# Overflow groups moved ahead of the third group, and the next layer's query weights and product moved ahead of expert 28, in a two-layer mixture-of-experts trunk

## The reference, cut to what matters

```
u   = rms_norm(x) @ w_in                 # 1024 x 3328, first 512 columns: attention queries
x   = x + mixer(u) @ w_out               # attention, gated recurrence, short convolution
h   = rms_norm(x)
g   = best of 4 groups;  e1, e2 = best 2 of the 8 experts in it    # per token
x   = x + sum over e1, e2 of gate_e * ((silu(h @ w_gate[e]) * (h @ w_up[e])) @ w_down[e])
```

## Time and profile before

| | us |
|---|---|
| three runs | 1174.75, 1175.57, 1178.22 (median 1175.57) |
| the profiled execution, whole | 1178.1 |
| its span, first to last instruction | 1176.3 |
| mean granted TensorE clock | 0.904 of full speed |

### The profile page before, as it was taken

How to read it: one execution, slowest core, us unless ns; L and a number is a source line. 1 busy time by engine, 2 the same in 40 slices (tenths; PEclk the granted TensorE clock), 3 DMA queues, 4 the chain that set the end, 5 groups by cost and what they waited for, 6 DMA issues and landing times.

```text
span 1176.3 us, 21016 instructions
## 1 busy us (share of the span) xinstructions
PE 891.2 (76%) x8821; PEld 539.1 (46%) x8821; DVE 473.4 (40%) x1264; ACT 181.8 (15%) x508; POOL 43.3 (4%) x98
## 2 busy tenths in 40 slices
PE   9999998665757665648999999886666667565577
PEld 6577475332424332325575675643323233333244
DVE  2977474331313132323349674733223222232322
ACT  2334121100101010001223441111000000000001
POOL 2001120000000000000000120000000000000000
PEclk9999999897979797988999999987978797989888
DMA  8946589999999999999996275999999999999996
GB/s 277 380 197 244 221 351 426 426 427 427 428 428 428 430 428 429 426 428 417 417 387 264 72 279 199 374 426 427 426 428 427 428 430 428 428 428 430 427 425 271
DMA packets 56147, 442.32 MB, mean 376 GB/s; under 512 B 9472, under 2 KB 12560, under 8 KB 31248
## 3 DMA queue, kind: packets, MB, share of 16 engines
q1 hardware_dynamic: 56080, 441.37, 91.1%
HBM read 440.30 MB, written 1.05 MB: 375 GB/s over the span
## 4 chain that ended last, share of the span: by engine, by line
PE 53%; DMA 38%; DVE 5%; issue 2%; SPq 1%; ACT 0%; DVEq 0%; POOL 0%; POOLq 0%
DMA ring<-in_expert_w_up 38%; PE psum L969 14%; PE psum L1002 8%; PE psum L1013 6%; PE psum L983 5%; PE psum L1088 5%; PE psum L780 2%; PE psum L942 2%; DVE work L1727 1%; PE psum L819 1%; PE psum L1036 1%; PE psum L870 1%; SPq L493 1%; PE psum L1271 1%; PE psum L959 1%
## 5 line engine op out<-in xcount | busy, mean ns | idle before, releaser
L969 PE MATMUL psum<-ring,work 128*32 128x256 f32 x3712 | 257.0, 438 | 111.7 <-DMA ring<-in_expert_w_up 111.2
L969 PEld LDWEIGHTS psum<-ring,work 128*32 128x32 f32 x3712 | 143.9, 126 | 221.8 <-issue 173.3
L983 PE MATMUL psum<-ring,work 128*32 128x256 f32 x1664 | 128.2, 461 | 127.7 <-DVE work L1733 127.5
L1725 DVE TENSOR_SCALAR work<-work 128x128 f32<-128x128 f32 x62 | 14.5, 233 | 346.1 <-ACT work L1357 346.1
L983 PEld LDWEIGHTS psum<-ring,work 128*32 128x32 f32 x1664 | 57.5, 129 | 193.2 <-DVE work L1733 117.3
L1738 DVE COPY work<-psum 32x256 f32<-32x256 f32 x124 | 52.6, 424 | 139.7 <-PE psum L983 138.6
L1002 PE MATMUL psum<-ring,hT 128*128 128x512 f32 x208 | 91.0, 593 | 0.0
L1361 ACT ACTIVATE work<-psum 32x256 f32<-32x256 f32 x124 | 46.3, 373 | 266.4 <-PE psum L983 265.7
L1357 ACT ACTIVATE work<-psum 128x128 f32<-128x128 f32 x62 | 17.2, 278 | 364.4 <-PE psum L969 333.6
L1013 PE MATMUL psum<-hT,ring 128*128 128x256 f32 x320 | 70.8, 379 | 0.0
L942 PE MATMUL psum<-work 128*128 128x512 f32 x112 | 53.4, 621 | 15.1 <-DVE work L1738 15.1
(11 more groups left out here) (321 smaller groups left out, 837.1 us busy)
## 6 DMA issues: line engine op xcount, KB each, us to landing
ring<-in_expert_w_gate SPq DMA_DIRECT2D x64, 2048.0 KB, 18.1
ring<-in_expert_w_up SPq DMA_DIRECT2D x60, 2048.0 KB, 22.5
ring<-in_expert_w_down SPq DMA_DIRECT2D x52, 2048.0 KB, 22.0
ring<-in_w_in SPq DMA_DIRECT2D x10, 2048.0 KB, 18.8
work<-in_expert_w_down SPq DMA_DIRECT2D x6, 2048.0 KB, 15.0
ring<-in_w_out SPq DMA_DIRECT2D x4, 2048.0 KB, 8.1
maps<-in_expert_w_down SPq DMA_DIRECT2D x2, 2048.0 KB, 9.2
ring<-in_expert_w_up SPq DMA_DIRECT2D x4, 1024.0 KB, 30.7
```

The source lines that it names most:

```text
L969: last = T.matmul(bank[GU_BANK[i % 2]][CAP * j:CAP * j + CAP, 0:2 * P], xg[:, k, CAP * i:CAP * i + CAP], gate_up[:, :, k, P * j:P * j + P] ...
L983: last = T.matmul(bank[5][CAP * q:CAP * q + CAP, 0:2 * P], actT[i % 2][:, CAP * j:CAP * j + CAP], down[j][:, 2 * P * q:2 * P * q + 2 * P], ...
```

## The change

The overflow block moves on every engine from behind group 6 to behind group 1, so ahead of group 2. It then runs, where it runs, before the sums are final, and the copies and seeds that put them back are gone. ScalarE and VectorE have group 1 written out ahead of it and loop over groups 2 to 6.

SyncE issues the four loads of the next layer's query weights before the first load of expert 28, in place of behind its third.

On TensorE the whole product ahead of the first 128 tokens comes before expert 28's gate/up product, and that of the second 128 is split around expert 28's down and expert 29's gate/up product. `project_rest(0)` comes behind it, and a wait for its copy (`rest_sb`) stands in front of expert 30. ScalarE's copies follow that order.

The diff, without the removal of the signal `again_x` and of the parameter `seed` of `experts`:

```diff
@@ -589,26 +588,26 @@
                 part(ring_full, seven[1], 7, 1)
                 e.wait_ge(main.ye_ps.sem, main.ye_ps.after(first + 1, 1))
                 part(ring_full, seven[2], 7, 2)
+                count, prior = extra_groups(e, l)
+                with e.If(count > 0):
+                    with e.Fori(0, count) as t:
+
+                        e.wait_ge(main.scat_ps.sem, main.scat_ps.after(l * GROUPS + 2, 0))
+                        for i in range(UG):
+                            ex = e.value_load(xinfo[0:1, l:l + 1, ds(t * UG + (2 + i), 1)], min_val=0, max_val=NE - 1)
+                            unit(xring_full, extra, prior + t, i, ex)
+
+                        e.wait_ge(extra.scat_ps.sem, extra.scat_ps.after(prior + t, 4))
+                        settle(e)
                 with e.Fori(2, GROUPS - 1) as g:
                     for i in range(UG):
                         unit(ring_full, main, l * GROUPS + g, i, g * UG + i)
 
-                count, prior = extra_groups(e, l)
-                with e.If(count > 0):
-                    with e.Fori(0, count) as t:
-
-                        e.wait_ge(main.scat_ps.sem, main.scat_ps.after(l * GROUPS + GROUPS - 1, 0))
-                        for i in range(UG):
-                            ex = e.value_load(xinfo[0:1, l:l + 1, ds(t * UG + (2 + i), 1)], min_val=0, max_val=NE - 1)
-                            unit(xring_full, extra, prior + t, i, ex)
-
-                        e.wait_ge(extra.scat_ps.sem, extra.scat_ps.after(prior + t, 4))
-                        settle(e)
                 last = l * GROUPS + GROUPS - 1
+                if l < DEPTH - 1:
+                    first_section(l + 1)
                 for i in range(UG - 1):
                     unit(ring_full, main, last, i, (GROUPS - 1) * UG + i, LAST, 3)
-                    if i == 0 and l < DEPTH - 1:
-                        first_section(l + 1)
                 sg, su, sd = placed(l, LAST[UG - 1])
                 e.wait_ge(main.gu_ps.sem, main.gu_ps.after(last, UG - 3))
                 part(ring_full, sg, NE - 1, 0)
@@ -832,13 +831,14 @@
                 gate_transposes(S, turn, True)
                 if ahead:
                     sums_transposed()
-                    for n in range(TI):
-                        expert_units(S, turn, [("up", n)], slots, loaded)
-                        project_ahead(n, range(0, KT // 2))
-                        expert_units(S, turn, [("down", n)], slots, loaded)
-                        project_ahead(n, range(KT // 2, KT)).then_inc(ahead_q_ps.sem, 1)
-                        if n == 0:
-                            project_rest(0)
+                    project_ahead(0, range(0, KT)).then_inc(ahead_q_ps.sem, 1)
+                    expert_units(S, turn, [("up", 0)], slots, loaded)
+                    project_ahead(1, range(0, KT // 2))
+                    expert_units(S, turn, [("down", 0), ("up", 1)], slots, loaded)
+                    project_ahead(1, range(KT // 2, KT)).then_inc(ahead_q_ps.sem, 1)
+                    project_rest(0)
+                    expert_units(S, turn, [("down", 1)], slots, loaded)
+                    e.wait_ge(rest_sb.sem, rest_sb.after(l, 1))
                     expert_units(S, turn, [("up", 2)], slots, loaded)
                     project_rest(1)
                     expert_units(S, turn, [("down", 2)], slots, loaded)
@@ -931,10 +931,6 @@
                     gate_transposes(S, turn)
                     expert_units(S, turn, order, slots, loaded)
                 e.wait_ge(S.gat_sb.sem, S.gat_sb.after(turn, 1))
-                if seed:
-                    e.wait_ge(again_x.sem, again_x.after(turn, 4))
-                    for n in range(4):
-                        T.matmul(bank[SUM_BANK[n]][:, :], ident[:, :], x[:, n // 2, n % 2 * 512:n % 2 * 512 + 512], start=True, stop=False)
                 e.wait_ge(S.ye_act.sem, S.ye_act.after(turn, 4))
                 e.wait_ge(S.ye_dve.sem, S.ye_dve.after(turn, 4))
                 for n in range(4):
@@ -1276,14 +1272,14 @@
                 experts(main, l * GROUPS + 1, IN_TURN, second, unit_loaded(1))
                 more = l < DEPTH - 1
                 count, prior = extra_groups(e, l)
+                with e.If(count > 0):
+                    with e.Fori(0, count) as t:
+                        e.wait_ge(main.scat_ps.sem, main.scat_ps.after(l * GROUPS + 2, 0))
+                        experts(extra, prior + t, IN_TURN, later, lambda s, i: xring_full[s].after(prior + t, 16 * (i // 2 + 1)))
                 with e.Fori(2, GROUPS - 2 if more else GROUPS - 1) as g:
                     experts(main, l * GROUPS + g, IN_TURN, later, turn_loaded(g))
                 if more:
                     experts(main, l * GROUPS + GROUPS - 2, IN_TURN, later, turn_loaded(GROUPS - 2), final=True)
-                with e.If(count > 0):
-                    with e.Fori(0, count) as t:
-                        e.wait_ge(main.scat_ps.sem, main.scat_ps.after(l * GROUPS + GROUPS - 1, 0))
-                        experts(extra, prior + t, IN_TURN, later, lambda s, i: xring_full[s].after(prior + t, 16 * (i // 2 + 1)), more, more)
                 last_experts(l, l * GROUPS + GROUPS - 1, final, unit_loaded(GROUPS - 1))
 
 
@@ -1321,20 +1317,23 @@
                 e.wait_ge(S.gat_ps.sem, S.gat_ps.after(turn, 1))
                 A(gat_both, bank[7][:, :], ACT.Copy).then_inc(S.gat_sb.sem, 1)
                 if ahead:
+                    def part_out(t):
+
+                        e.wait_ge(ahead_q_ps.sem, ahead_q_ps.after(l, t + 1))
+                        A(part_q[t], bank[7][:, :], ACT.Copy).then_inc(ahead_q_sb.sem, 1)
+
+                    part_out(0)
                     for n in range(UG - 1):
                         expert_units(S, turn, [("up", n)])
-                        if n == 2:
-                            rest_out(1)
+                        if n == 1:
+                            part_out(1)
+                        if n:
+                            rest_out(n - 1)
                         e.wait_ge(S.ye_ps.sem, S.ye_ps.after(turn, n + 1))
                         if n:
                             e.wait_ge(yt_ok.sem, yt_ok.after(l, n))
                         A(flat[0:P // 2, :], bank[5][0:P // 2, 0:2 * P], ACT.Copy).then_inc(flat_ok.sem, 1)
                         expert_units(S, turn, [("down", n)])
-                        if n < TI:
-                            e.wait_ge(ahead_q_ps.sem, ahead_q_ps.after(l, n + 1))
-                            A(part_q[n], bank[7][:, :], ACT.Copy).then_inc(ahead_q_sb.sem, 1)
-                        if n == 0:
-                            rest_out(0)
                 else:
                     expert_units(S, turn, LAST_TURN)
                 e.wait_ge(gate_ps.sem, gate_ps.after(l, 1))
@@ -1526,18 +1525,14 @@
                 A(edif, edif, ACT.Exp).then_inc(exp_e.sem, 1)
 
                 experts(main, l * GROUPS, OVERLAPPED)
-
-                with e.Fori(1, GROUPS - 1) as g:
-                    experts(main, l * GROUPS + g, IN_TURN)
+                experts(main, l * GROUPS + 1, IN_TURN)
                 count, prior = extra_groups(e, l)
                 with e.If(count > 0):
                     with e.Fori(0, count) as t:
-                        e.wait_ge(main.scat_ps.sem, main.scat_ps.after(l * GROUPS + GROUPS - 1, 0))
-                        if l < DEPTH - 1:
-                            sums_to_x(again_x)
+                        e.wait_ge(main.scat_ps.sem, main.scat_ps.after(l * GROUPS + 2, 0))
                         experts(extra, prior + t, IN_TURN)
-                        if l < DEPTH - 1:
-                            e.wait_ge(extra.scat_ps.sem, extra.scat_ps.after(prior + t, 4))
+                with e.Fori(2, GROUPS - 1) as g:
+                    experts(main, l * GROUPS + g, IN_TURN)
                 last_experts(l, l * GROUPS + GROUPS - 1)
 
 
@@ -2178,12 +2173,13 @@
                 experts(main, l * GROUPS, OVERLAPPED, codes, l, l * (GROUPS - 1), extra_units, gate_values)
                 c.end()
                 e.wait_ge(c.sem, c.last())
-                with e.Fori(1, GROUPS - 1) as g:
-                    experts(main, l * GROUPS + g, IN_TURN, codes, l, l * (GROUPS - 1) + g)
+                experts(main, l * GROUPS + 1, IN_TURN, codes, l, l * (GROUPS - 1) + 1)
                 count, prior = extra_groups(e, l)
                 with e.If(count > 0):
                     with e.Fori(0, count) as t:
                         experts(extra, prior + t, IN_TURN, xcodes, l, prior + t)
+                with e.Fori(2, GROUPS - 1) as g:
+                    experts(main, l * GROUPS + g, IN_TURN, codes, l, l * (GROUPS - 1) + g)
                 last_experts(l, l * GROUPS + GROUPS - 1)
 
 
```

More of the change, by code:

```diff
@@ L332, in hybrid_trunk @@
         flat_ok, yt_ok, rest_ps, rest_sb = sig("flat_ok", 3), sig("yt_ok", 4), sig("rest_ps", 4), sig("rest_sb", 4)
-        again_x = sig("again_x", 4)
         dve_ahead = sig("dve_ahead", DVE_AHEAD)
```

(12 more changed lines are left out.)

## The result

| | us |
|---|---|
| before, 16 runs | 1174.23 to 1180.3, median 1176.89 |
| after, 16 runs | 1175.82 to 1181.88, median 1179.9 |
| ratio after to before | 1.0021, 95% interval 1.0011 to 1.0031 |

By the ratio that is 2.5 us lost (1.3 to 3.6), where 3.5 us gained were forecast. The two profiled executions (1178.1 before, 1177.6 after, span 1175.8) happen to lie the other way: single executions of either kernel spread over 6 us, so the profiles are used for where time goes, and the ratio for how much.

A forecast was written before the change was run, and what follows sets the result against it. TensorE (53%) and DMA (38%) were taken to bound the kernel in turns. -4.3 us at layer 0's last group and +0.8 for the new jump gave -3.5, from a median of 1175.57 to 1172.0 us; range 1169.3 to 1177.5.

The forecast's parts named there:

- The jump put in between group 1 and group 2: Ahead of group 2: gap and slow gather delay expert 10's weights 5.8 us, leaving a 0.8 us hole in layer 1.
- the two old jumps: TensorE's jumps over the skipped block before group 7, one per layer: gaps of 3.11 and 2.71 us, gathers 6.56 and 6.76.
- the 5 us that the prediction named as a sign of being wrong: TensorE's gap in front of group 2: the prediction is wrong if it exceeds 5 us.
- The same in layer 0: Layer 0's new jump ahead of group 2: same delay, taken as 5.8 us, within 9.3 us of slack.
- The rival of the costly new jump: Ahead of group 2: two fetches and slow products delay 11.1 us, holes 6.1 and 1.8, so 1179.2 us; chance 0.10.
- The jump taken away in front of group 7: Layer 0, TensorE: gap gone (3.28 us) and gather back to 3.73 us (2.83), together 6.11 us gained.
- The exposed copy ahead of the product: Layer 0, ahead of expert 28: first query product waits for VectorE's copy into hT, about 0.8 us lost.
- Where the data stop it: Layer 0, expert 30: its up weights' landing lets only 4.3 of the 5.3 us gain arrive.
- The short gap at 590: Layer 0's last group: 1.16 us issue gap, left in the forecast; its loss would add 1.2 us of gain.
- Query weights in front: Layer 0, ahead of expert 28's loads: same bytes through a full queue, cost 0.
- the stuck-SyncE case: Layer 0: SyncE held 34 us in query DMAs before issuing expert 28, some 6 us missing in the stream.
- End of layer 1: Jump taken away there saves TensorE 5.7 us but only lengthens expert 29's 2.87 us wait for data: 0.

The follow-up runs named there:

- experiment 3: Changed kernel without the overflow groups' code on any engine, so no jump over it in either layer; 0.9946 (0.9926 to 0.9966) of the kernel before.
- experiment 4: Changed kernel with the overflow block's body cut to one instruction on every engine, test and branch kept; 0.9940 (0.9919 to 0.9961) of the kernel before.
- experiment 5: Changed kernel with never-executed filler in TensorE's skipped block, 90 instructions in layer 0 and 190 in layer 1; 0.9971 (0.9957 to 0.9985) of the kernel before.
- experiment 6: Changed kernel with never-executed filler in TensorE's skipped block, 70 instructions in layer 0 and 210 in layer 1; 1.0003 (0.9991 to 1.0016) of the kernel before.
- experiment 8: Changed kernel with layer 1's block behind group 6 again and 90 never-executed fillers in layer 0's block on TensorE; 0.9951 (0.9932 to 0.9969) of the kernel before.

## Why the prediction was wrong

- **The jump put in between group 1 and group 2** is the step that failed. The mechanism was as put: a gap, late issue of expert 10's weights, a hole where the slack runs out. The slack was about right (9.3 and 5.0 us). What was mis-sized is the delay in layer 1: I took 5.8 us from the two old jumps. From the scatter's start to the issue of expert 10's gate it grew from 834.20 - 820.95 = 13.25 to 840.21 - 817.14 = 23.07 there, which is 9.8, with 2.33 + 4.96 = 7.3 us idle, beyond the 5 us that the prediction named as a sign of being wrong. The hole became 7.0 in place of 0.8. The rest of it: relative to TensorE the stream stood 1.5 us earlier than before (expert 8's gate weights issued at 801.11 and landed 11.6 later, before at 804.86 and 13.1 later), which leaves 3.5 of the slack, and the landing took 8.9 in place of 8.1: 9.8 - 3.5 + 0.8 = 7.1.
- **The same in layer 0** grew from 11.25 to 255.52 - 236.58 = 18.94, which is 7.7. But 2.2 of that is the slow scatter, which is not the jump's, so the jump cost 5.5 there, near the 5.8 forecast. The hole was 1.2 in place of 0: the stream stood 1.1 us earlier against the scatter and the landing took 9.8 in place of 8.1, so 7.7 + 1.1 + 1.7 - 9.3 = 1.2. Behind both old jumps the gather ran in one piece, so they gave no price for a jump with a second gap.
- **The rival of the costly new jump** (0.10) was what happened, with its delay of 11.1 near the 9.8 seen in layer 1. Its reason was half right: there are two stalls, but the second goes with the target's place among the instructions and not with the loop (experiments 3 to 6). That its sum came so close is partly luck, since nothing in the change chose that place: experiments 5 and 6 differ only in 20 instructions that never run, moved from one block to the other.
- **The jump taken away in front of group 7**: right. Gap gone, gather 3.73, clock full (1.00 in 535 to 539.5). The nine instruction packets of the earlier trace rows did not yet tie the gap to the jump; experiments 3 and 4 do. The Trainium skill (page "Runtime: NRT & Kernel Launch", "Instruction fetch mechanics") says that a taken branch to a target outside the fetched window waits for a fetch, without a duration; the trace agrees, with 2.2 to 5.1 us here. The Trainium skill's other page, "Advanced Engine Details and Errata" ("Control Flow Timing"), gives a compare-and-branch about 108 ns; that is compatible only with the near branch of experiment 4, where no gap shows.
- **The exposed copy ahead of the product**: 0.8 forecast, 0.79 measured.
- **Where the data stop it**: I held the gain at 4.3 and it was 7.2. The short gap at 590 was gone (1.2); expert 30's weights landed at 527.91 + 42.8 = 570.7, which is 38.5 us behind group 6's scatter against 39.9 before, so the cap was 1.4 higher; the rest is small. In experiments 3 and 8, where expert 30 did wait 2.3 us, the gain was 4.7 and 3.7: the cap of 4.3 was a fair figure, and the 7.2 also depends on how far TensorE is behind the stream when it gets there.
- **Query weights in front**: 0 forecast; no difference that can be told. SyncE was free again at 524.0, so the stuck-SyncE case did not arise.
- **End of layer 1**: 0, as forecast. The gather was early by the gap, and expert 29 waited 5.53 us in place of 2.87.

The sum from the profiles is -7.2 + 1.2 + 7.0 = +1.0 against +2.5 (1.3 to 3.6) by the ratio. It has the sign right and lies just below the interval; the missing 1.5 us was not traced.

## What to carry to other kernels

A test over a block that is almost never taken can still cost the engine that jumps over it: here 2.2 to 5.1 us of silence, at times 5 us more, and behind most of the gaps a gather at a granted clock of some 0.5 to 0.7. Put it where that engine waits for data anyway, and look at that place's slack in each pass, not at the average. Where it must stand on the bounding path, keep the skipped code short, or see how many instructions run behind the target before the next gap. A gap that moves when never-executed code changes length comes of where the code lies and not of what it does, and the measurement of one layout doesn't give its size.

## What the runs showed of the hardware

TensorE's first gap behind a far jump ranged from 2.20 to 5.05 us over the layouts tried; what sets its size is open. When the target lay three to six L779 records ahead of a break, a second gap of 4.96 to 5.07 us followed (three layouts), with an instruction packet falling within the second gap. With 39 records in between, the second gap was 1.17 us. A jump over a block of one instruction showed no gap. That the gaps are fetches of instructions is inferred: they come with the far jump, they move with code that never runs, and packets on the instruction queue fall in them; the profile itself puts them down to issue.
